# Three-branch attention layers and a mixture of experts on one core: the output gate's modulation weights are loaded and summed during attention instead of among the projections

## The chip, the cores and the metric

The kernel runs on one core of one Trainium2 chip, in float32. The metric is the device time of one execution in microseconds (us), as the median of three runs. TensorE (PE) multiplies and writes into eight banks of on-chip memory (`banks` in the trace), everything else lies in one large buffer (`arena`). VectorE (DVE), ScalarE (ACT) and GpSimd (POOL) work beside it, and SyncE (SP) issues nearly all of the weight loads.

## The reference, cut to what matters

Two layers of the first kind (`DEPTH = 2`), then one block of a second kind that ends in a mixture of experts. The change touches only the two layers. `x` is 256 tokens by 1024, and `gate` is one row of 1024 numbers for all tokens.

```python
for l in range(DEPTH):
    mod = c_act @ w_ada[l] + b_ada[l]
    shift, scale, gate = [m[:, None, :] for m in split_cols(mod, (D, D, D))]
    h = rms_norm(x, g_pre[l]) * (1.0 + scale) + shift
    (cq, ckv, kr, za, qb_, kb_, vb_, zb, qc, kc, vc, zc, gcols) = split_cols(h @ w_in[l], IN_SPLITS)
    o_a = (mla_branch(cq, ckv, kr, g_q[l], w_uq[l], g_kv[l], w_ukv[l], cos, sin)
           * jax.nn.silu(za)) @ w_o_mla[l]
    o_b = (swa_branch(qb_, kb_, vb_, sink[l], swa_bias) * jax.nn.silu(zb)) @ w_o_swa[l]
    o_c = (diff_branch(qc, kc, vc, ..., rel_bias, lam_init) * jax.nn.silu(zc)) @ w_o_diff[l]
    g = jax.nn.sigmoid(gcols).reshape(B, S, N_BRANCH, D)
    y = (g[:, :, 0] * o_a + g[:, :, 1] * o_b + g[:, :, 2] * o_c) @ w_out[l]
    x = x + gate * rms_norm(y, g_post[l])
```

## The kernel before

**A layer has four stages.** First x is transposed and scaled (jobs `xT`). Then come the projections that attention needs (jobs `cq`, `ckv`, `qb`, `kb`, `vb`, `qr`, `qn`, `qc`, `kn`, `kc`, `v`, `vc`). Then attention itself, 24 units of which each is a head or half of one (8 sliding-window, 8 differential, 8 latent), runs in 25 ticks (`TICKS`). In each tick PE does the scores, transposes or values of a unit and in between a piece of the fill: the jobs from `z` to the last `g`, with `ada` and `modT`, the next layer's shift and scale. `share` deals the fill out over the ticks by a cost per job, a quarter of a `z` or `g` job being the smallest piece. Last come the output products (`wo`, `wout`) and the new x. In the first layer the projections lie at 42 to 147 us of the trace and attention at 148 to 327 us, in the second at 408 to 505 us and from 506 us on.

**Jobs and banks.** `layer_jobs` writes the order of the jobs on PE by hand. Job number n uses one of three banks in turn; it waits until the engine that read job n-3 has let the bank go.

**Loads and slots.** `layer_loads` writes the order in which SP issues the weight loads (L776), each of at most 128 partitions x 2048 numbers (1 MB), into a ring of six slots. Load i goes into the slot of load i-6, so SP waits until the last job that uses load i-6 is done (`LAST_USER`), and since SP works in order, all loads behind it wait too. A projection of 512 columns takes two loads, for input rows 0 to 511 and 512 to 1023.

**The gate.** `gate` is made on DVE, not on PE: four loads (`mods_now`, two for each half of the rows, 4 MB in all) are multiplied row tile by row tile with the condition's column and summed into `mrow` (`gate_rows`, L719 and L725: 16 instructions of 128x512). Half 1 is summed before DVE reads `qr`, half 2 after it has copied `kc` 0. The slots of these loads come free by DVE's signals `gate_read` and `gate_sum`. Two PE jobs `gate` (L858, a product with a matrix of ones) then add over the partitions, and DVE turns the result with `row_b` (bias) and `row_g` (the post-norm weights) into `G1` (L1370, L1372), which is used at the layer's end. `row_g` lies in `pT`, the buffer into which attention copies transposed probabilities, so G1 must be done before attention.

**Softmax chain in a tick.** DVE scales the scores and takes the maximum (`before_exp`, L1404 to L1410), ACT does the exponentials (L1129), DVE normalises (L1420 to L1445), PE transposes in the next tick (L956). Scores of units u and u+1 (L946) are computed together in even ticks and wait until the exponentials of unit u-1 are done.

Of the kernel before, what the change touches and what calls it, by code (L numbers as in the profile page):

```python
# [42 lines left out]
def layer_loads():  # L43
# [10 lines left out]
    for c in (4, 5):  # L54
        loads.append(("mods_now", 0, 4, 512 * c, 512))
# [26 lines left out]
def layer_jobs():  # L82

    jobs = []
    for i in range(4):
# [7 lines left out]
    i += 4  # L93
    uq, qc, ukv, kc, vc = (i,), (i + 1, i + 2), (i + 3,), (i + 6, i + 7), (i + 8, i + 9)
    i += 10
    jobs += [("qr", 0, uq), ("qn", 0, uq), ("qc", 0, qc), ("qn", 1, uq), ("qc", 1, qc), ("kn", 0, ukv),
             ("kc", 0, kc), ("kn", 1, ukv), ("kc", 1, kc), ("v", 0, ukv), ("v", 1, ukv), ("gate", 0, ()),
             ("vc", 0, vc), ("gate", 1, ()), ("vc", 1, vc)]
    for z in range(3):
        jobs += [("z", 2 * z, (i, i + 1)), ("z", 2 * z + 1, (i, i + 1))]  # L100
        i += 2
# [43 lines left out]
TICKS = NU + 1  # L145

# [12 lines left out]
def share(jobs, first, last, parts, t):  # L159
# [3 lines left out]
    for j in range(first, last):  # L163
        cost = {"ada": 1 / 3, "mod": 1 / 3, "modT": 1 / 10, "modT2": 1 / 10}.get(jobs[j][0])
# [20 lines left out]
def fill_jobs(t):  # L185

    return finished(fill_shares(t))
# [317 lines left out]
def blocks_kernel(nc, A, out):  # L505
# [4 lines left out]
    with ExitStack() as ctx:  # L510
# [82 lines left out]
        row_b, row_g = spare[:, 0:D], pT  # L593
# [115 lines left out]
        def gate_rows(dve, loads, half, turns, cond, acc):  # L709
# [70 lines left out]
        def _(pe):  # L780
# [31 lines left out]
            for l in range(LAYERS):  # L812
# [25 lines left out]
                def job(j, quarters=WHOLE):  # L838
# [17 lines left out]
                    elif kind == "gate":  # L856
                        pe.wait_ge(gate_sum.sem, gate_sum.at(l, n + 1))
                        mm = pe.matmul(b, C("ones"), mrow[:, 512 * n:512 * n + 512], start=True, stop=True)  # L858
# [184 lines left out]
        def _(act):  # L1043
# [16 lines left out]
            act.dma_start(row_b, A["b_ada"][0:1, 2 * D:3 * D].to_broadcast([P, D])).then_inc(rows_in, 16)  # L1060
            act.dma_start(row_g, A["g_post"][0:1, :].to_broadcast([P, D])).then_inc(rows_in, 16)

            for l in range(LAYERS):
# [18 lines left out]
                copy_job(j, cq, bank_of(l, j))  # L1082
                j = JOB_OF["ckv", 0]
# [55 lines left out]
                for t in range(TICKS):  # L1139
# [10 lines left out]
                    for j in fill_jobs(t):  # L1150
                        kind, n, _ = JOBS[j]
                        if kind == "modT":
                            continue
# [20 lines left out]
                if l < LAYERS - 1:  # L1174
                    act.dma_start(lv, A["lvecs"][l + 1]).then_inc(lv_in, 16)
                    act.dma_start(row_b, A["b_ada"][l + 1:l + 2, 2 * D:3 * D].to_broadcast([P, D])).then_inc(rows_in, 16)
                    act.dma_start(row_g, A["g_post"][l + 1:l + 2, :].to_broadcast([P, D])).then_inc(rows_in, 16)
# [1580 lines left out]
```

## Time and profile before

| | |
|---|---|
| time, median of three runs (lowest to highest) | 2347.01 us (2346.2 to 2348.6) |
| the profiled execution: its time, its span in the trace | 2345.47 us, 2343.7 us |
| PE matmul busy | 1808.4 us, 77% |
| DVE busy | 524.9 us, 22% |
| ACT busy | 287.4 us, 12% |
| the chain that ended last, shares of the span | PE 48%, DMA 46%, DVE 3% |
| PE waiting for `w_in` loads at L830, whole run | 7.6 us |

The page cuts the span into 40 slices of 58.6 us. In slices 2 to 19, PE is busy for nine tenths or more nearly throughout and the DMA queues for two to seven tenths. From slice 20 on it is the other way round: the experts' weights stream in at 427 to 430 GB/s with the DMA nine tenths busy, and PE waits. The chain that ended last shows the same: PE lines up to about 1110 us, then loads of the experts' weights. A view "in order of time" lists start, duration, what; a bracket gives the idle time before it and who ended it. In these views one matmul of float32 shows as two records, so a job of 16 matmuls is x32.

### The profile page before, as it was taken

The page shows a single profiled execution, that of the slowest core. Times are in us where ns is not written, and L with a number is a line of the kernel's source. Part 1 is how long each engine was busy: PE and PEld are TensorE (multiplying, and loading weights), DVE is VectorE, ACT ScalarE, POOL GpSimd, SP SyncE. Part 2 cuts the span into 40 slices and gives each one's busy share as a digit, 9 for nine tenths or more (in the row PEclk, how much of TensorE's full clock was granted, in tenths as well). Part 3 has the DMA queues.
Part 4 walks back from the last instruction along what each step waited for, and adds up shares of the span by engine and source line. Part 5 has one row for each costly group of instructions (what it writes and reads, how often), then busy time and mean ns, then how long its engine had stood idle before and what let it go on. Part 6 is the DMA issues. An engine that isn't in the chain of part 4 may idle for free.

```text
span 2343.7 us, 23974 instructions
## 1 busy us (share of the span) xinstructions
PE 1808.4 (77%) x10388; PEld 1018.3 (43%) x10388; DVE 524.9 (22%) x1136; ACT 287.4 (12%) x710; POOL 61.9 (3%) x101
## 2 busy tenths in 40 slices
PE   6999999999999999989666575656666665666666
PEld 3767785867786677554212121212221222222212
DVE  1234323234313337753000010000010000000001
ACT  1122211113220112311000000000000000000001
POOL 1000000000000300110000000000000000000000
PEclk9999999999999999999878787877787877788778
DMA  9664453443464341378999999999999999999996
GB/s 301 214 202 144 171 181 112 150 175 138 171 222 135 123 144 37 106 289 363 427 428 425 429 429 427 425 430 428 427 427 429 428 427 428 429 427 427 429 428 265
DMA packets 126223, 714.38 MB, mean 305 GB/s; under 512 B 11545, under 2 KB 16089, under 8 KB 96303
## 3 DMA queue, kind: packets, MB, share of 16 engines
q1 hardware_dynamic: 117568, 697.07, 73.4%
q10 hardware_dynamic: 6279, 9.88, 1.3%
q0 software_dynamic: 2272, 5.90, 1.1%
q8 instruction: 83, 1.36, 0.2%
q14 instruction: 21, 0.17, 0.0%
HBM read 709.02 MB, written 3.80 MB: 304 GB/s over the span
## 4 chain that ended last, share of the span: by engine, by line
PE 48%; DMA 46%; DVE 3%; SPq 1%; ACT 1%; issue 1%; POOL 0%; DVEq 0%; ACTq 0%
DMA arena<-in_w_up_dram 22%; DMA arena<-in_w_down_dram 20%; PE banks L830 14%; PE banks L2547 5%; PE banks L1723 4%; PE banks L918 4%; PE banks L1732 3%; PE banks L2579 2%; PE banks L926 2%; DMA arena<-in_w_mods_dram 2%; PE banks L2587 2%; PE banks L835 2%; DMA arena<-in_w_in_dram 1%; PE banks L946 1%; PE banks L1765 1%; PE banks L974 1%
## 5 line engine op out<-in xcount | busy, mean ns | idle before, releaser
L2547 PE MATMUL banks<-arena 128*32 128x512 f32 (+2 forms) x3072 | 418.1, 682 | 330.1 <-DMA arena<-in_w_up_dram 330.1
L2547 PEld LDWEIGHTS banks<-arena 128*32 128x32 f32 x3072 | 131.5, 132 | 587.1 <-issue 579.7
L830 PE MATMUL banks<-arena 128*128 128x256 f32 x1536 | 346.7, 382 | 7.6 <-DMA arena<-in_w_in_dram 7.6
L830 PEld LDWEIGHTS banks<-arena 128*128 128x128 f32 x1536 | 287.9, 191 | 50.3 <-DMA arena<-in_w_in_dram 8.8
L2579 PE MATMUL banks<-arena 128*32 128x512 f32 x1280 | 205.0, 792 | 95.2 <-DMA arena<-in_w_down_dram 95.2
L2675 DVE SCALAR_TENSOR_TENSOR arena<-arena,banks 64x512 f32<-64x512 f32 (+1 forms) x48 | 30.5, 635 | 517.9 <-ACT arena L2598 516.9
L2579 PEld LDWEIGHTS banks<-arena 128*32 128x32 f32 x1280 | 44.3, 132 | 229.9 <-DMA arena<-in_w_down_dram 129.7
L2598 ACT ACTIVATE arena<-banks 64x512 f32<-64x512 f32 (+1 forms) x48 | 26.6, 555 | 818.9 <-PE banks L2547 817.6
L1723 PE MATMUL banks<-arena 128*128 128x256 f32 x512 | 113.7, 380 | 1.4 <-DVE arena L2120 0.7
L1723 PEld LDWEIGHTS banks<-arena 128*128 128x128 f32 x512 | 95.9, 190 | 16.1 <-issue 3.8
L2682 DVE COPY arena<-banks 128x512 f32<-128x512 f32 x16 | 11.1, 692 | 350.1 <-PE banks L2588 350.1
L918 PE MATMUL banks<-arena 128*128 128x256 f32 x384 | 83.4, 379 | 1.7 <-DVE arena L1482 1.7
L918 PEld LDWEIGHTS banks<-arena 128*128 128x128 f32 x384 | 72.8, 190 | 12.3 <-issue 2.5
L1732 PE MATMUL banks<-arena 128*128 128x512 f32 x160 | 69.8, 593 | 0.0
L2668 DVE COPY arena<-banks 128x256 f32<-128x256 f32 x16 | 6.8, 425 | 258.4 <-PE banks L2485 258.4
L2498 PE MATMUL banks<-arena 128*128 128x512 f32 x128 | 60.0, 611 | 0.8 <-ACT arena L2612 0.8
L926 PE MATMUL banks<-arena 128*128 128x512 f32 x128 | 55.4, 593 | 3.5 <-DVE arena L1501 3.5
L2551 PE MATMUL banks<-arena 128*32 128x128 f32 x512 | 55.3, 295 | 0.0
L2516 PE MATMUL banks<-arena 64*128 64x64 f32 x176 | 30.1, 289 | 31.0 <-DVE arena L2677 31.0
L2612 ACT COPY arena<-banks 128x512 f32<-128x512 f32 x16 | 9.4, 585 | 327.9 <-PE banks L2588 327.9
L1129 ACT ACTIVATE arena<-arena 128x256 f32<-128x256 f32 x64 | 32.0, 500 | 118.1 <-DVE arena L1410 67.9
L2551 PEld LDWEIGHTS banks<-arena 128*32 128x32 f32 x512 | 34.4, 123 | 27.0 <-issue 8.9
(334 smaller groups left out, 1688.6 us busy)
## 6 DMA issues: line engine op xcount, KB each, us to landing
arena<-in_w_gate_dram SPq DMA_DIRECT2D x60, 2752.0 KB, 35.7
arena<-in_w_up_dram SPq DMA_DIRECT2D x60, 2752.0 KB, 32.7
arena<-in_w_down_dram SPq DMA_DIRECT2D x64, 2048.0 KB, 32.0
arena<-in_w_in_dram SPq DMA_DIRECT2D x68, 1024.0 KB, 7.7
arena<-in_w_mods_dram SPq DMA_DIRECT2D x48, 1024.0 KB, 7.3
arena<-in_w_down_dram SPq DMA_DIRECT2D x32, 1024.0 KB, 27.0
arena<-in_w_out_dram SPq DMA_DIRECT2D x12, 1024.0 KB, 5.7
arena<-in_w_gate_dram SPq DMA_DIRECT2D x8, 1376.0 KB, 9.6
```

The source lines that it names most:

```text
L830: mm = pe.matmul(b[:, i * S:i * S + S], w, rhs[:, kt, :], start=kt == 0, stop=kt == 7)
L835: mm = pe.matmul(outp, cols(slot(i0 + kt // 4)[:, kt % 4, :]), rhs[:, kt, :], start=kt == 0, stop=kt == 7)
L918: mm = pe.matmul(b[:, i * S:i * S + S], w[:, k, c:c + P], zv[:, 4 * br + k, :], start=k == 0, stop=k == 3)
L926: mm = pe.matmul(b, hTv[:, kt, t * P:t * P + P], slot(loads[0] + kt // 4)[:, kt % 4, :], start=kt == 0, stop=kt == 7)
L1129: ins = nc.scalar.activation(Ev[:, u % 3, t * S:t * S + S], src, ACT.Exp, bias=nmx[:, u % 3, t:t + 1], scale=QK ** -0.5 if kind == "mla" e ...
L1723: mm = pe.matmul(b[:, i * S:i * S + S], slot(loads[kt // 4])[:, kt % 4, c0:c0 + P], rhs[:, kt, :], start=kt == 0, stop=kt == 7)
L1732: mm = pe.matmul(b, lhs[:, kt, (n % 2) * P:(n % 2) * P + P], slot(loads[kt // 4])[:, kt % 4, :], start=kt == 0, stop=kt == 7)
L2498: mm = pe.matmul(acc[2 * t + c], GT[:, e % 2, t * P:t * P + P], Y[:, 512 * c:512 * c + 512], start=e == 0, stop=e == NE - 1, skip_group_ch ...
L2547: mm = pe.matmul(bank[pc][32 * g:32 * g + 32, 0:w_], xsT[:, kt, CAP * e4:CAP * e4 + CAP], (wg if g < 2 else wu)[:, c:c + w_], start=kt == ...
L2551: mm = pe.matmul(bank[pc][32 * g:32 * g + 32, LAST - c0:w], xsT[:, kt, CAP * e4:CAP * e4 + CAP], (wg if g < 2 else wu)[:, FF - 64:FF].unsq ...
L2579: mm = pe.matmul(bank[c][32 * g:32 * g + 32, :], hTv3[:, j, 32 * hf:32 * hf + 32], w_[:, 512 * c:512 * c + 512], start=(g, c) not in start ...
L2587: pe.matmul(bank[c][0:32, :], hTv3[:, 10, 0:32], lo[:, 512 * c:512 * c + 512], start=False, stop=True)
```

## The change

It moves the four `mods_now` loads from among the projections to behind the loads of `zb` and `zc`; moves the summation on DVE into attention's ticks 1, 2 (half 1) and 4, 5 (half 2); moves the two `gate` jobs on PE behind the `z` jobs, into the fill (tick 7); and moves the making of G1 there too. The sums are kept in `xn[:, 0:D]`, the buffer of the normalised x, which is idle between `xT` and the layer's end, and `row_g` in its other half. So `mrow` and `pT` are free of them, and both rows are loaded in each layer by ACT after its copy of `cq`, instead of before the first layer and after attention.

```diff
@@ layer_loads
     chunk("w_in", D, COL["kb"], 256)
-    for c in (4, 5):
-        loads.append(("mods_now", 0, 4, 512 * c, 512))
     loads.append(("w_uq", 0, 2, 0, MLA_H * QK))
     chunk("w_in", D, COL["qc"], 512)
     loads.append(("w_ukv", 0, 1, 0, MLA_H * (NOPE + VD)))
-    for c in (4, 5):
-        loads.append(("mods_now", 512, 4, 512 * c, 512))
...
     for z in ("zb", "zc", "za"):
         chunk("w_in", D, COL[z], 512)
+        if z != "za":
+            for c in (4, 5):
+                loads.append(("mods_now", 0 if z == "zb" else 512, 4, 512 * c, 512))
@@ layer_jobs
-             ("kc", 0, kc), ("kn", 1, ukv), ("kc", 1, kc), ("v", 0, ukv), ("v", 1, ukv), ("gate", 0, ()),
-             ("vc", 0, vc), ("gate", 1, ()), ("vc", 1, vc)]
+             ("kc", 0, kc), ("kn", 1, ukv), ("kc", 1, kc), ("v", 0, ukv), ("v", 1, ukv),
+             ("vc", 0, vc), ("vc", 1, vc)]
...
+    jobs += [("gate", n, ()) for n in range(2)]
...
+GATE_TICKS = {1: (1, (0, 1)), 2: (1, (2, 3)), 4: (2, (0, 1)), 5: (2, (2, 3))}
@@ share
-        cost = {"ada": 1 / 3, "mod": 1 / 3, "modT": 1 / 10, "modT2": 1 / 10}.get(jobs[j][0])
+        cost = {"ada": 1 / 3, "mod": 1 / 3, "modT": 1 / 10, "modT2": 1 / 10, "gate": 1 / 10}.get(jobs[j][0])
@@ buffers
-        row_b, row_g = spare[:, 0:D], pT
+        row_b, row_g, gate_acc = spare[:, 0:D], xn[:, D:2 * D], xn[:, 0:D]
@@ gate_rows
-            for i in both:
-                dve.wait_ge(ring_full[(MOD_LOADS + i) % RING], 16 * (turns + (MOD_LOADS + i) // RING + 1))
-            for k in range(4):
+            if part[0] == 0:
+                for i in both:
+                    dve.wait_ge(ring_full[(MOD_LOADS + i) % RING], 16 * (turns + (MOD_LOADS + i) // RING + 1))
+            for k in part:
@@ ACT, in each layer between its copy of cq and its copy of ckv (and no longer ahead of
@@ layer 0 and behind attention)
+                act.dma_start(row_b, A["b_ada"][l:l + 1, 2 * D:3 * D].to_broadcast([P, D])).then_inc(rows_in, 16)
+                act.dma_start(row_g, A["g_post"][l:l + 1, :].to_broadcast([P, D])).then_inc(rows_in, 16)
@@ DVE, projections
-                gate_rows(dve, GATE_LOADS, 1, l * (NLOAD // RING), 0, mrow)
...
-                        if n == 0:
-                            gate_rows(dve, GATE_LOADS, 2, l * (NLOAD // RING), 0, mrow)
@@ DVE, in each tick, behind before_exp and normalise
+                    if t in GATE_TICKS:
+                        half, part = GATE_TICKS[t]
+                        gate_rows(dve, GATE_LOADS, half, l * (NLOAD // RING), 0, gate_acc, part)
                     for j in fill_jobs(t):
...
+                        if kind == "gate":
+                            a = slice(512 * n, 512 * n + 512)
+                            dve.wait_ge(job_done.sem, made(l, j))
+                            dve.wait_ge(rows_in, 32 * l + 32)
+                            nc.vector.tensor_tensor(row_b[:, a], bank_of(l, j), row_b[:, a], ALU.add).then_inc(v_own.sem, v_own.up())
+                            dve.wait_ge(v_own.sem, v_own.last())
+                            nc.vector.scalar_tensor_tensor(G1[:, a], row_b[:, a], 0.5, row_g[:, a], ALU.mult, ALU.mult).then_inc(reader(l, j), 1)
```

The loads on SP's queue, from the first layer's `kb` (128x4x256) to the loads of the first `g` jobs, before:

```order
L776 DMA arena<-in_w_in_dram 128x4x256 x2
L776 DMA arena<-in_w_mods_dram 128x4x512 x2
L776 DMA arena<-in_w_uq_dram 128x2x768
L776 DMA arena<-in_w_in_dram 128x4x512 x2
L776 DMA arena<-in_w_ukv_dram 128x1024
L776 DMA arena<-in_w_mods_dram 128x4x512 x2
L776 DMA arena<-in_w_in_dram 128x4x512 x12
```

and in the changed kernel:

```order
L778 DMA arena<-in_w_in_dram 128x4x256 x2
L778 DMA arena<-in_w_uq_dram 128x2x768
L778 DMA arena<-in_w_in_dram 128x4x512 x2
L778 DMA arena<-in_w_ukv_dram 128x1024
L778 DMA arena<-in_w_in_dram 128x4x512 x6
L778 DMA arena<-in_w_mods_dram 128x4x512 x2
L778 DMA arena<-in_w_in_dram 128x4x512 x2
L778 DMA arena<-in_w_mods_dram 128x4x512 x2
L778 DMA arena<-in_w_in_dram 128x4x512 x4
```

The x6 are `kc`, `vc` and `zb`; then stand the gate's half 1, `zc`, the gate's half 2, `za` and the first `g`. So every load from `w_uq` to `zb` now goes into the slot of a load that stands six useful loads ahead of it.

DVE in tick 1 and the start of tick 2 of the first layer's attention, before (score scaling, maximum, normalising, then the `z` job's gating at L1469):

```order
L1404 SCALAR_TENSOR_TENSOR arena<-banks,arena 128x256
L1405 SCALAR_TENSOR_TENSOR arena<-banks,arena 128x256
L1407 TENSOR_REDUCE arena<-arena 128x2
L1410 TENSOR_SCALAR arena<-arena 128x2
L1420 TENSOR_TENSOR arena<-arena 128x2
L1422 RECIPROCAL arena<-arena 128x2
L1445 TENSOR_SCALAR arena<-arena 128x256 x2
L1469 SCALAR_TENSOR_TENSOR arena<-arena,banks 128x512
L1404 SCALAR_TENSOR_TENSOR arena<-banks,arena 128x256
```

and in the changed kernel:

```order
L1393 SCALAR_TENSOR_TENSOR arena<-banks,arena 128x256
L1394 SCALAR_TENSOR_TENSOR arena<-banks,arena 128x256
L1396 TENSOR_REDUCE arena<-arena 128x2
L1399 TENSOR_SCALAR arena<-arena 128x2
L1409 TENSOR_TENSOR arena<-arena 128x2
L1411 RECIPROCAL arena<-arena 128x2
L1434 TENSOR_SCALAR arena<-arena 128x256 x2
L721 TENSOR_SCALAR arena<-arena 128x512 x2
L727 SCALAR_TENSOR_TENSOR arena<-arena 128x512 x2
L1468 SCALAR_TENSOR_TENSOR arena<-arena,banks 128x512
L1393 SCALAR_TENSOR_TENSOR arena<-banks,arena 128x256
```

Four instructions of the gate's sum (L721, L727) stand behind the unit's normalising and ahead of the `z` job's gating. The same holds in ticks 2, 4 and 5, with four of L727 each.

PE at the end of the projections, before (`v` at L906, `gate` at L858, `vc` at L886, the first scores at L946):

```order
L906 MATMUL banks<-arena 128x512 x2
L858 MATMUL banks<-arena 128x512
L886 MATMUL banks<-arena 128x512 x8
L858 MATMUL banks<-arena 128x512
L886 MATMUL banks<-arena 128x512 x8
L946 MATMUL banks<-arena 128x256 x4
```

and in the changed kernel:

```order
L908 MATMUL banks<-arena 128x512 x2
L888 MATMUL banks<-arena 128x512 x16
L948 MATMUL banks<-arena 128x256 x4
```

The two `gate` jobs have left this place; they stand in tick 7, behind the last `z` job and ahead of the scores of tick 8.

## Rows read from the trace of the kernel before

**Rows 1.** The page, part 2: PE's busy tenths in 40 slices of the span

```profile
PE   6999999999999999989666575656666665666666
```

**Rows 2.** PE in order of time, layer 0's projections: start, us, what, [idle before]

```profile
86.76 1.89 PE L830 MATMUL banks<-arena 128*128 128x256 f32 x8
91.91 5.45 PE L830 MATMUL banks<-arena 128*128 128x256 f32 x24 [3.25 <-DMA arena<-in_w_in_dram]
97.19 1.90 PE L896 MATMUL banks<-arena 128*128 128x256 f32 x8
98.92 7.07 PE L830 MATMUL banks<-arena 128*128 128x256 f32 x32
...
106.94 1.99 PE L830 MATMUL banks<-arena 128*128 128x256 f32 x8
...
116.52 1.08 PE L902 MATMUL banks<-arena 128*64 128x256 f32 x8
...
127.12 3.60 PE L886 MATMUL banks<-arena 128*128 128x512 f32 x8
134.41 5.40 PE L886 MATMUL banks<-arena 128*128 128x512 f32 x8 [3.70 <-DMA arena<-in_w_in_dram]
139.65 1.02 PE L858 MATMUL banks<-arena 128*128 128x512 f32 x2
140.51 7.03 PE L886 MATMUL banks<-arena 128*128 128x512 f32 x16
```

**Rows 3.** The same view, layer 1's projections

```profile
467.67 1.99 PE L830 MATMUL banks<-arena 128*128 128x256 f32 x8
471.79 7.13 PE L830 MATMUL banks<-arena 128*128 128x256 f32 x24 [2.12 <-DMA arena<-in_w_in_dram]
478.85 1.08 PE L902 MATMUL banks<-arena 128*64 128x256 f32 x8
...
489.45 3.59 PE L886 MATMUL banks<-arena 128*128 128x512 f32 x8
...
497.51 1.02 PE L858 MATMUL banks<-arena 128*128 128x512 f32 x2
```

**Rows 4.** Stretches: length, busy PE, PEld, DVE, ACT, POOL, granted clock, DMA share, GB/s

```profile
134.00:137.00 3.00, 2.58 (x4) 1.07 (x5) 0.00 (x0) 0.00 (x0) 0.00 (x0) 0.61 1.05 385
...
470.00:475.00 5.00, 3.21 (x9) 2.60 (x10) 0.00 (x0) 0.00 (x0) 0.00 (x0) 0.76 0.81 304
```

**Rows 5.** SP's queue in order of time: the two loads of `qc`, layer 0

```profile
73.94 9.13 SPq L776 DMA_DIRECT2D arena<-in_w_in_dram  x2
```

**Rows 6.** The line of the weight loads (L776), 60 to 160 us: issue to landing

```profile
DMA to landing us min/median/max: 4.8/7.6/14.9
```

**Rows 7.** DVE in order of time: the gate's sums in layer 0

```profile
88.14 4.06 DVE L725 SCALAR_TENSOR_TENSOR arena<-arena 128x512 f32<-128x512 f32 x6
...
117.35 5.39 DVE L725 SCALAR_TENSOR_TENSOR arena<-arena 128x512 f32<-128x512 f32 x8
```

**Rows 8.** DVE in order of time, attention: tick 2 starts, tick 2 ends

```profile
161.54 0.42 DVE L1404 SCALAR_TENSOR_TENSOR arena<-banks,arena 128x256 f32<-128x256 f32 x1 [3.20 <-PE banks L946]
...
168.45 0.42 DVE L1482 SCALAR_TENSOR_TENSOR arena<-banks,arena 128x256 f32<-128x256 f32 x1 [1.53 <-PE banks L974]
```

**Rows 9.** ACT in order of time: unit 3's last exponential (tick 3)

```profile
171.55 0.28 ACT L1133 ACTIVATE arena<-arena 128x2 f32<-128x2 f32 x1
```

**Rows 10.** PE in order of time: the scores of tick 4, which wait for it

```profile
174.00 1.14 PE L946 MATMUL banks<-arena 64*128 64x256 f32 x8
```

**Rows 11.** POOL in order of time: the root made at the end of tick 13

```profile
244.94 0.70 POOL L1225 TENSOR_TENSOR arena<-arena 128x2 f32<-128x2 f32 x1 [13.85 <-DVE arena L1458]
```

**Rows 12.** PE in order of time: the product in tick 14 that needs it

```profile
247.41 0.61 PE L1030 MATMUL banks<-arena 128*128 128x128 f32 x4
```

**Rows 13.** ACT in order of time: its copy of `ckv` in layer 0

```profile
56.31 0.37 ACT L1085 COPY arena<-banks 128x256 f32<-128x256 f32 x1 [6.43 <-PE banks L835]
```

**Rows 14.** What SP's queue waited for, 850 to 1200 us: us in total, times, longest

```profile
SPq L2441 <- PE banks L1765: 27.8, 1, 27.8
```

More of the change, by code:

```diff
@@ L92, in layer_jobs @@
     jobs += [("kb", 0, (i, i + 1)), ("vb", 0, (i, i + 1))]
[L93 to L95 removed]
+    i += 2
+    uq, qc, ukv, kc, vc = (i,), (i + 1, i + 2), (i + 3,), (i + 4, i + 5), (i + 6, i + 7)
+    i += 8
     jobs += [("qr", 0, uq), ("qn", 0, uq), ("qc", 0, qc), ("qn", 1, uq), ("qc", 1, qc), ("kn", 0, ukv),
[L97 to L98 removed]
+             ("kc", 0, kc), ("kn", 1, ukv), ("kc", 1, kc), ("v", 0, ukv), ("v", 1, ukv),
+             ("vc", 0, vc), ("vc", 1, vc)]
     for z in range(3):
         jobs += [("z", 2 * z, (i, i + 1)), ("z", 2 * z + 1, (i, i + 1))]
[L101 removed]
+        i += 4 if z < 2 else 2
+    jobs += [("gate", n, ()) for n in range(2)]
     for g in range(6):
@@ L707, in taken, with gate_rows @@
             return place(l, j) // BANKS + 2
-        def gate_rows(dve, loads, half, turns, cond, acc):
+        def gate_rows(dve, loads, half, turns, cond, acc, part=range(4)):
             both = [i for i, n in sorted(loads.items()) if n == half]
-            for i in both:
-                dve.wait_ge(ring_full[(MOD_LOADS + i) % RING], 16 * (turns + (MOD_LOADS + i) // RING + 1))
-            for k in range(4):
+            if part[0] == 0:
+                for i in both:
+                    dve.wait_ge(ring_full[(MOD_LOADS + i) % RING], 16 * (turns + (MOD_LOADS + i) // RING + 1))
+            for k in part:
                 for c, i in enumerate(both):
@@ L857, in job @@
                         pe.wait_ge(gate_sum.sem, gate_sum.at(l, n + 1))
-                        mm = pe.matmul(b, C("ones"), mrow[:, 512 * n:512 * n + 512], start=True, stop=True)
+                        mm = pe.matmul(b, C("ones"), gate_acc[:, 512 * n:512 * n + 512], start=True, stop=True)
                     elif kind == "xT":
@@ L1151, in _ @@
                         kind, n, _ = JOBS[j]
-                        if kind == "modT":
+                        if kind in ("modT", "gate"):
                             continue
@@ L1360, in _ @@
                 dve.wait_ge(v_own.sem, v_own.last())
-                gate_rows(dve, GATE_LOADS, 1, l * (NLOAD // RING), 0, mrow)
-                dve.wait_ge(rows_in, 32 * l + 32)
                 for kind, n, _ in MIDDLE:
-                    if kind not in ("kc", "qr", "gate"):
+                    if kind not in ("kc", "qr"):
                         continue
@@ L1367, in _ @@
                     dve.wait_ge(job_done.sem, made(l, j))
-                    if kind == "gate":
-                        a = slice(512 * n, 512 * n + 512)
-                        nc.vector.tensor_tensor(row_b[:, a], bank_of(l, j), row_b[:, a], ALU.add).then_inc(v_own.sem, v_own.up())
-                        dve.wait_ge(v_own.sem, v_own.last())
-                        nc.vector.scalar_tensor_tensor(G1[:, a], row_b[:, a], 0.5, row_g[:, a], ALU.mult, ALU.mult).then_inc(reader(l, j), 1)
-                        continue
                     if kind == "kc":
                         nc.vector.tensor_copy(kcT[:, 512 * n:512 * n + 512], bank_of(l, j)).then_inc(reader(l, j), 1)
-                        if n == 0:
-                            gate_rows(dve, GATE_LOADS, 2, l * (NLOAD // RING), 0, mrow)
                         continue
```

4 lines of the change are left out of this document (removed).

## The prediction, made before the changed kernel was run

> **What bounds the kernel now.** I read the page's slices first: PE is busy nine tenths of nearly all of slices 1 to 18, then only five to seven tenths [rows 1]. So up to about 1110 us PE's order of work is the path, and behind it the experts' weights stream in. The question for the tail is whether a head start reaches the end. SP's first loads of those weights wait 27.8 us for PE's line L1765 [rows 14]: the stream is started by PE's progress, not by a clock of its own. Whatever PE gains in the layers, the stream should start that much earlier, and the end moves one for one.
>
> Second, PE in order of time over the projections. In layer 0 it stands still three times in the middle of a job, always for the job's second `w_in` load: in `qc` 0 (3.25 us, behind 86.76), `kc` 0 (behind 106.94) and `vc` 0 (3.70 us) [rows 2]. Layer 1 shows two, in `kc` 0 (2.12 us) and `vc` 0 [rows 3]. Attention behind it has nearly no waits.
>
> Third, why those loads are late. It isn't bandwidth: landing takes 4.8 us at best, 7.6 in the middle [rows 6]. It is the slots. The two `w_in` loads of `qc` take 9.13 us to issue [rows 5]: the first goes out at 73.94, when `qb` is done, and the second at 73.94 + 9.13 = 83.1, because its slot belongs to `kb` and `vb` must be done with it. Its job resumes at 91.91 [rows 2]. The second load of `vc` waits for the slot of `w_ukv`, free when `v` 1 is done just before 127.1, and its job resumes at 134.41 [rows 2]. The code says why the slots are short: two of the six hold gate weights, first half 1, then half 2, and these come free only by DVE.
>
> **Part 1, the stalls go.** I price each job by its start and the start of the next row, against a job without a stall: 7.07 us for L830 x32, 7.03 for `vc` x16 [rows 2]. `qc` 0: 97.19 - 86.76 = 10.43, too long by 3.36. `kc` 0: 116.52 - 106.94 = 9.58, by 2.51. `vc` 0: 139.65 - 127.12 = 12.53, by 5.50. Layer 0: 11.37 us. Layer 1 [rows 3]: `kc` 0 478.85 - 467.67 = 11.18, by 4.11; `vc` 0 497.51 - 489.45 = 8.06, by 1.03; together 5.14 us. The sum is **16.5 us**.
>
> It holds more than the waits, since the granted clock was 0.61 in 134 to 137 us and 0.76 in 470 to 475 [rows 4]: behind a stall some matmuls ran at the lower level of 1.2 GHz. Eight records took 5.40 instead of 3.60 us, and 24 took 7.13 instead of 5.45 [rows 2, 3]. Behind the 3.25 us wait in `qc` 0, the 24 records took 5.45, no such loss. The Trainium skill (TensorE: Matmul & The Clock Gate, Why this matters for your kernels) asks for matmul bursts without long idle gaps and says that a gap long enough drops the clock. The trace agrees for 3.70 us and not for 3.25, while 2.12 us in layer 1 did cost it; priced by the rule alone, the 3.25 us gap would add some 1.7 us to the sum, which the row denies.
>
> **Do the new slots come free in time?** I walk the new order with the old times, less what is saved by then. The second `qc` load now takes a slot of `qb`, free at 73.9 us [rows 5], and is needed at 86.76 + 1.89 = 88.7 [rows 2]: 14.8 us. Both `kc` loads take `kb`'s slots, free at 83.1 [rows 5], and the first is needed at 106.94 - 3.36 = 103.6: 20 us. The second `vc` load takes a slot of `qc`, free when `qc` 1 is done at 98.92 + 7.07 - 3.36 = 102.6, and is needed at 127.12 - 5.87 - 0.86 + 3.6 = 124.0 (5.87 for the two stalls before it, 0.86 for the `gate` job that leaves, 140.51 - 139.65 [rows 2]): 21 us. The second `zb` load takes `w_ukv`'s slot at about 120.4 and is needed some 17 us later, behind two `vc` jobs of 7.03, the first scores and a first quarter job. The worst landing was 14.9 [rows 6]. Projections: no stall left.
>
> **Part 2, the gate loads.** The ticks' times first, by the old clock: DVE's tick 1 ends at 161.54 - 3.20 = 158.3 [rows 8]; PE's tick 2 begins 1.14 us ahead of 161.54, at 160.4, and its tick 4 at 174.00 [rows 10], so a tick is 6.8 us. Now half 1: it is issued behind `zb` at 121 us, and DVE asks for it at 158 less the 13.1 us by which attention starts earlier (11.4 and the two `gate` jobs' 1.7), so at 145: 24 us for three loads. Half 2 takes `zb`'s slots when `z` 1 is done in tick 2, two quarter jobs and the transposes behind the scores, at 160.4 + 1.1 + 0.6 + 3.6 = 165.7, and is wanted in tick 4 some 5 us behind its scores, at 179: 13 us. `za` waits for DVE's `gate_read` at the end of its tick 2 (168.5) and is needed by PE in tick 5, at 174.0 + 6.8 + 0.6 + 1.8 = 183.2: 15 us. These two are the tight ones, with nearly twice the median landing.
>
> **Part 3, the sums on DVE.** Eight instructions take 5.39 us [rows 7], so a tick gets 2.7 us. Nothing is added, it is moved; in the projections it hid behind PE. In tick 1 the 3.20 us idle takes it [rows 8]. In tick 2 the 1.53 us idle and 0.6 us more take all but 0.6 us of it [rows 8], so unit 3's exponential ends at 171.83 + 0.6 = 172.4 [rows 9]; the scores that need it start at 174.00 [rows 10]. Cover left: 1.6 us. Ticks 4 and 5 hold the same instructions, and the new deal of the fill gives PE a quarter job more in tick 5. **Cost 0**; without the cover a tick would cost up to 2.7 us.
>
> **Part 4, PE's gate jobs and G1.** The same two jobs, moved: 0. In tick 7 DVE adds four steps of about 0.68 us (4.06 / 6 [rows 7]), 2.7 us ahead of tick 8, whose exponentials no PE work needs before tick 9: 0. DVE also waits there for the two rows, which ACT has issued more than 100 us before.
>
> **Part 5, the row loads on ACT.** They stand between the copies of `cq` and `ckv`, where ACT idles 6.43 us for PE [rows 13]; two issues under 1 us hide there: 0. Their 1 MB now travels with the `w_uq` and `qc` loads, which the Trainium skill (DMA: Bandwidth & Descriptors, Issuing engines are not separate DMA queues) says share the same 16 engines whoever issues. No row prices that here; by it `qc` would land a few us later, inside its 15 us.
>
> **Part 6, the fill is dealt anew.** The costs of two `gate` jobs shift pieces between ticks. Tick 13 loses one quarter job, 1.8 us of PE. At its end PE needs a root that POOL makes at 244.94 + 0.70 = 245.64, for L1030 at 247.41 [rows 11, 12]. Less 1.8 that is 245.6, so a wait of 0.1 to 0.4 us, in both layers. I take **0.5 us lost**; bounds 0 and 2 (a whole POOL step and its signals in each layer).
>
> **The sum.** 16.5 - 0.5 = 16.0 us off the profiled 2345.47: 2329.5. The median is 1.54 us above the profiled run, so **2331 us**.
>
> **Rivals.** *A new late load in attention.* `za` or gate half 2 misses by a landing near 14.9 us [rows 6], PE stalls some 2 us in tick 4 or 5 and pays the clock's 1.8 us again, in both layers: about 8 us lost, **2339 us**. For: SP's order puts DVE's `gate_read` ahead of all later loads. Against: both have 13 us or more and the median is 7.6 [rows 6].
>
> *The stalls only move (the change doesn't do what it says).* If transfer speed and not slots set the arrivals, dropping 4 MB out of the stretch would still leave waits, since `zb` follows at once: half of the gain, 2339, or none, **2347**. Against: the 9.13 us issue [rows 5] is a slot wait.
>
> *Slower: the sums enter the softmax chain.* All 16 sums and the four steps of G1 on the path would be 20 x 0.68 = 13.5 us a layer, 27 in both, less 16.0: **2358 us**. It decides when DVE's delay at tick 4's scores passes the 1.6 us left, or the gate's weights land more than 24 us after issue, so that DVE stands in tick 1 with the `z` gating and unit 2's score scaling queued behind it, and PE's transposes of unit 2 in tick 3 wait for those. Against: DVE's idle in each tick.
>
> **How the numbers follow.** Forecast 0.80 (2327 to 2335: the sum with part 6's bounds, and 1 to 2 us for run to run and for a stall priced by one execution). New late load 0.10 (2335 to 2343). Stalls move 0.06 (2339 to 2347). Sums on the path 0.04. The range 2326 to 2339 holds the forecast and most of the second case. A measurement of this kernel can tell about 0.2%, 4.7 us, from no change: faster 0.93, same 0.04, slower 0.03.
>
> **What would show it.** Right: no wait of PE for `in_w_in_dram` in either layer's projections, granted clock 1.00 there, attention starting near 135 us instead of 148 in layer 0 and near 488 instead of 506 in layer 1, and the experts' first loads 16 us earlier. Wrong: waits of L830 in ticks 4 or 5 for a load, of L946 for ACT or DVE in ticks 2 to 6, or an end that moved less than the experts' first load.

## The result, and the profile after

| | before | after |
|---|---|---|
| median (lowest to highest) | 2347.81 us (2346.2 to 2348.95, 4 runs) | 2329.27 us (2327.31 to 2330.87, 4 runs) |
| ratio after to before, 95% interval | | 0.9922 (0.991 to 0.9934) |
| span of the profiled execution | 2343.7 us | 2327.4 us |
| PE matmul busy | 1808.4 us | 1809.7 us |
| DVE, ACT busy | 524.9, 287.4 us | 523.9, 287.3 us |

The forecast was 2331 us. The medians are 18.5 us apart, the two profiled executions 16.3 us, where the prediction's sum was 16.0. No engine has less work (PE's busy time differs by 1.3 us, DVE's by 1.0): what went is idle time.

PE in the page's slices, to be held against [rows 1]. Only four slices have another digit, each by one tenth and all in the experts' part: at 58 us a slice, waits of 1 to 4 us don't show, and these digits alone would say that nothing happened:

```profile
PE   6999999999999999989666566656665666666666
```

PE's costliest line in the layers, from the page. It does the same 1536 records in 343.4 us (346.7 before, where some of them ran at the lower clock), and the idle time ahead of it, 7.6 us for loads before, is 0:

```profile
L832 PE MATMUL banks<-arena 128*128 128x256 f32 x1536 | 343.4, 380 | 0.0
```

PE in order of time over the projections of layer 0 (start, duration, what), which answers to [rows 2]:

```profile
86.51 7.07 PE L832 MATMUL banks<-arena 128*128 128x256 f32 x32
...
103.17 7.17 PE L832 MATMUL banks<-arena 128*128 128x256 f32 x32
...
118.30 1.88 PE L908 MATMUL banks<-arena 128*128 128x512 f32 x4
120.01 13.90 PE L888 MATMUL banks<-arena 128*128 128x512 f32 x32
134.69 1.14 PE L948 MATMUL banks<-arena 64*128 64x256 f32 x8 [0.78 <-ACT arena L1067]
```

`qc` 0 (86.51) is one unbroken row of 32 records (before 8, a wait, 24), so is `kc` 0 (103.17), and `vc` 0 and 1 are one row of 13.90 us. The first scores start at 134.69 instead of 148.32. Layer 1, against [rows 3] (`kc` 0 lies at 455.87, 7.17 us, unbroken too):

```profile
472.72 13.90 PE L888 MATMUL banks<-arena 128*128 128x512 f32 x32
487.39 1.14 PE L948 MATMUL banks<-arena 64*128 64x256 f32 x8 [0.78 <-ACT arena L1067]
```

And the granted clock (the column PEclk, here the 1.00 behind POOL's) over both stretches, which was 0.61 and 0.76 in places before [rows 4]:

```profile
core 0: us, PE busy (x) PEld busy (x) DVE busy (x) ACT busy (x) POOL busy (x), PEclk, DMA share, GB/s
60.00:135.00 75.00, 74.22 (x337) 56.16 (x337) 11.74 (x20) 11.87 (x21) 4.85 (x7) 1.00 0.68 205
425.00:490.00 65.00, 64.22 (x290) 48.03 (x289) 13.10 (x23) 9.22 (x16) 0.00 (x0) 1.00 0.48 164
```

How much earlier each point of the program is reached, from the views in order of time (* not in the rows above or in those of before):

| | before | after | earlier by |
|---|---|---|---|
| layer 0, first scores | 148.32* | 134.69 | 13.6 |
| layer 0, first `wo` | 327.68* | 315.87* | 11.8 |
| layer 1, first scores | 506.18* | 487.39 | 18.8 |
| layer 1, first `wo` | 685.54* | 668.58* | 17.0 |
| experts' first load issued | 1041.00* | 1024.10 | 16.9 |
| end of the span | 2343.7 | 2327.4 | 16.3 |

The experts' first load, before and after, in SP's queue in order of time:

```profile
1041.00 0.34 SPq L2441 DMA_DIRECT2D arena<-in_w_gate_dram  x1
1024.10 0.34 SPq L2440 DMA_DIRECT2D arena<-in_w_gate_dram  x1
```

Each attention is 1.8 us longer, which is the two `gate` jobs moved into it.

### The profile page after: what moved, and what is told of

The parts are those of the page before. It is cut to its first block, busy times and chain, and to the rows that moved or that the text cites. A ratio compares the mean times of both kernels' runs of the same rounds, so it can differ in the third digit from the quotient of the medians.

```text
span 2327.4 us, 23978 instructions
## 1 busy us (share of the span) xinstructions
PE 1809.7 (78%) x10388; PEld 1019.3 (44%) x10388; DVE 523.9 (23%) x1136; ACT 287.3 (12%) x710; POOL 61.8 (3%) x101
## 4 chain that ended last, share of the span: by engine, by line
PE 49%; DMA 44%; DVE 3%; SPq 1%; ACT 1%; issue 1%; POOL 0%; DVEq 0%; ACTq 0%
DMA arena<-in_w_up_dram 22%; DMA arena<-in_w_down_dram 21%; PE banks L832 14%; PE banks L2546 5%; PE banks L1722 4%; PE banks L920 4%; PE banks L1731 3%; PE banks L928 2%; PE banks L2578 2%; DMA arena<-in_w_mods_dram 2%; PE banks L2586 2%; PE banks L837 2%; PE banks L948 1%; PE banks L1764 1%; PE banks L888 1%; PE banks L976 1%
## 5 line engine op out<-in xcount | busy, mean ns | idle before, releaser
L832 PE MATMUL banks<-arena 128*128 128x256 f32 x1536 | 343.4, 380 | 0.0
L832 PEld LDWEIGHTS banks<-arena 128*128 128x128 f32 x1536 | 287.3, 190 | 39.7 <-issue 3.0
L920 PEld LDWEIGHTS banks<-arena 128*128 128x128 f32 x384 | 72.8, 190 | 12.3 <-issue 2.5
```

The source lines that it names most:

```text
L832: mm = pe.matmul(b[:, i * S:i * S + S], w, rhs[:, kt, :], start=kt == 0, stop=kt == 7)
L920: mm = pe.matmul(b[:, i * S:i * S + S], w[:, k, c:c + P], zv[:, 4 * br + k, :], start=k == 0, stop=k == 3)
```

## The experiments

**Theory:** the gate loads cost time by the places that they take in the ring's order, not by their bytes and not by DVE's lateness. **Rivals:** transfer speed; DVE's late release; and, for what the new place costs, a softmax chain on the edge. Ratios are to the kernel before, run on the same chip beside it; differences to after in microseconds are between medians that may come from different chips.

**1. Same places, next to no bytes.** The gate weights are cut to 16 of 512 columns, so most of them are left out.

```diff
@@ before: SP's loop over the loads
+                    if name == "mods_now":
+                        w = 16
                     sp.dma_start(view(ring[:, s_, 0:k * w], k, w), ...)
```

> The kernel before, except that each of the four gate loads of a layer brings 16 columns instead of 512 (32 KB instead of 1 MB); the slots, their order and DVE's sums stay, so most of the gate's weights are left out. Theory (slots: a load waits until the load six places ahead of it is used up, and gate loads take two of the six places): the second halves of qc, kc and vc still land late, PE still waits some 9 us in layer 0 and 3 us in layer 1, and the time is within 3 us of before. Rival (transfer speed: 4 MB more in the projections delay the others): PE's waits for w_in go, and the time falls by 10 to 17 us.

Measured: 2348.36 us, ratio 1.0003 (0.9993 to 1.0012). PE's waits, from the view of waits in 40 to 700 us:

```profile
PE banks L832 <- DMA arena<-in_w_in_dram: 7.6, 3, 3.4
PE banks L888 <- DMA arena<-in_w_in_dram: 4.7, 2, 3.9
```

Four MB fewer per layer and all five waits are still there, 12.3 us of them. It is the places.

**2. The bytes without the places.** The kernel after, with 3.5 MB per layer of loads that nobody reads, into idle buffers outside the ring, issued by SP among the projections' loads; ACT and DVE wait for them ahead of attention.

```diff
@@ after: SP's loop, ahead of load 6 and of load 10 of each layer
+                    if i == 6:
+                        for dst in (G[:, 4096:6144], zs[:, 0:2048]):
+                            sp.dma_start(view(dst, 4, 512), dram("mods_now", l, 0, 4, 2048, 512)).then_inc(extra_in, 16)
+                    if i == 10:
+                        for dst in (zs[:, 2048:3072], pT, mrow):
+                            sp.dma_start(view(dst, 2, 512), dram("mods_now", l, 512, 2, 2048, 512)).then_inc(extra_in, 16)
```

> The changed kernel with 3.5 MB of extra loads per layer that nobody reads, issued where the gate's halves stood before (2 MB behind kb's loads, 1.5 MB behind w_ukv's), into buffers that attention fills only later, so into no slot of the ring. Theory (slots): PE has no wait for w_in in the projections, attention starts within 1 us of the changed kernel's 134.7 us, and the time is within 2 us of it. Rival (transfer speed): waits of several us come back in qc or kc, and the time rises by 5 to 17 us.

Measured: 2329.0 us, ratio 0.9922 (0.9906 to 0.9937), the same as after. The windows (DMA share is the second last column), first of this kernel, then of after:

```profile
55.00:65.00 10.00, 10.00 (x48) 7.42 (x47) 0.16 (x1) 1.67 (x4) 1.04 (x1) 1.00 0.94 295
...
85.00:95.00 10.00, 10.00 (x48) 8.79 (x47) 6.97 (x9) 1.76 (x3) 0.00 (x0) 1.00 0.94 312
```

```profile
55.00:65.00 10.00, 10.00 (x48) 7.50 (x47) 0.16 (x1) 1.67 (x4) 2.62 (x3) 1.00 0.74 256
...
85.00:95.00 10.00, 10.00 (x48) 8.79 (x47) 6.83 (x9) 1.76 (x3) 0.00 (x0) 1.00 0.70 232
```

The DMA engines are busy for 0.94 of both stretches, after's for 0.74 and 0.70, and PE is full in them; it has no wait for `w_in` in the layers, and the first scores start at 134.82. With 1 and 2 the rival of transfer speed is out from both sides.

**3. One half back.** The kernel after with the two loads of half 1 back behind `kb`'s and summed there; half 2 stays in attention, and the job indices and `GATE_TICKS` follow.

```diff
@@ after: layer_loads
     chunk("w_in", D, COL["kb"], 256)
+    for c in (4, 5):
+        loads.append(("mods_now", 0, 4, 512 * c, 512))
...
-        if z != "za":
+        if z == "zc":
             for c in (4, 5):
-                loads.append(("mods_now", 0 if z == "zb" else 512, 4, 512 * c, 512))
+                loads.append(("mods_now", 512, 4, 512 * c, 512))
@@ DVE, projections
+                gate_rows(dve, GATE_LOADS, 1, l * (NLOAD // RING), 0, gate_acc)
```

> The changed kernel with half 1 of the gate put back: its two loads stand behind kb's again and DVE sums it ahead of qr; only half 2 is loaded behind zc and summed in ticks 4 and 5. Theory (slots): load i waits for load i-6, so the second qc load waits for vb again and PE waits 3 to 4 us in qc 0 of layer 0 (start to start 10.4 instead of 7.0 us), nothing in kc 0 or vc 0 and nothing in layer 1; the time is 3.4 us above the changed kernel. Rival (each half costs the same): half of the gain is lost, 8 us above it.

Measured: 2336.86 us, ratio 0.995 (0.9933 to 0.9967), 7.6 us above after. The only wait of PE for `w_in` in the layers, and the row behind it, in order of time:

```profile
86.86 1.89 PE L834 MATMUL banks<-arena 128*128 128x256 f32 x8
93.41 7.65 PE L834 MATMUL banks<-arena 128*128 128x256 f32 x24 [4.66 <-DMA arena<-in_w_in_dram]
100.90 1.90 PE L900 MATMUL banks<-arena 128*128 128x256 f32 x8
```

The place was foreseen (`qc` 0, and none in `kc` and `vc`), the price was not: 100.90 - 86.86 = 14.04, too long by 7.0 where [rows 2] gave 3.36. The job resumed 1.5 us later than there (93.41 against 91.91), after a wait of 4.66 us, which is longer than `qc` 0's in any execution of before or of experiments 1 and 4 (3.15 to 3.61) and wasn't explained, and the 24 records behind took 7.65 instead of 5.45. These 7.0 us are nearly the 7.6 measured, so half 1 alone makes `qc` 0's stall, and the other four waits need half 2's places (whether half 2 makes them alone wasn't run). The price differs between executions: one of the four runs took 2332.4 us, the others 2336.8 to 2337.1.

**4. Free the same places earlier.** The kernel before, with half 1's sums ahead of a wait in DVE's program, so that its slots come free earlier. No work is left out.

```diff
@@ before: DVE, projections
+                gate_rows(dve, GATE_LOADS, 1, l * (NLOAD // RING), 0, mrow)
                 dve.wait_ge(misc_done.sem, misc_done.at(l, 2))
...
-                gate_rows(dve, GATE_LOADS, 1, l * (NLOAD // RING), 0, mrow)
```

> The kernel before, except that DVE sums half 1 of the gate as soon as it has landed (near 62 us, where DVE is idle) instead of at 87 us, so that its two slots come free some 20 us earlier. Rival (the slots come free late because DVE is late): the waits of qc and kc in layer 0 go and the time falls by 5 to 9 us. Theory (the places in the order count, not how long DVE holds them): the late second loads wait for vb, qc 1 and v 1, which are PE's jobs, so all three waits stay and the time is within 2 us of before.

Measured: 2348.4 us, ratio 1.0002 (0.9993 to 1.0012). The wait in `qc` 0 stays, as do the other four (PE waits 12.2 us for `w_in` in all, as in before):

```profile
91.69 7.13 PE L830 MATMUL banks<-arena 128*128 128x256 f32 x24 [3.15 <-DMA arena<-in_w_in_dram]
```

It isn't how late DVE reads half 1. The late loads wait for the slots of `kb`, `qc` and `w_ukv`, six places back in the order, as the prediction's walk says for the first and the last of them.

**5. Fill two waits.** The kernel before, with matmuls that nobody reads between the halves of `vc` 0 (layer 0) and `kc` 0 (layer 1), to price the low clock behind a wait by itself.

```diff
@@ before: PE, job vc
                         for kt in range(8):
+                            if kt == 4 and l == 0 and n == 0:
+                                turn_over(pe, SB[0], 4)
@@ PE, job kc 0 of layer 1, between the quarters of its first and second load
+                            turn_over(pe, SB[0], 2)
```

> The kernel before with matmuls whose result nobody reads put into two of the waits: four of 128x512 (3.6 us at full clock) in vc 0 of layer 0, whose wait was 3.7 us, and two (1.8 us) in kc 0 of layer 1, whose wait was 2.1 us. Theory (1.7 us of each of these two stalls was the lower clock behind it, not the wait): the clock stays at 1.00, the matmuls behind the waits take 3.6 instead of 5.4 us and 5.4 instead of 7.1 us, and attention of layer 1 starts 3.5 us earlier than before. Rival (only the wait itself costs, the slow records are those of a late load): no change, within 0.5 us in the trace.

Measured: 2345.52 us, ratio 0.9989 (0.998 to 0.9998). The rows at the two places:

```profile
130.74 3.60 PE L748 MATMUL banks<-arena 128*128 128x512 f32 x8
134.38 3.70 PE L890 MATMUL banks<-arena 128*128 128x512 f32 x8
...
467.77 1.88 PE L748 MATMUL banks<-arena 128*128 128x512 f32 x4
470.07 5.45 PE L832 MATMUL banks<-arena 128*128 128x256 f32 x24 [0.42 <-DMA arena<-in_w_in_dram]
```

L748 is the filler. The loads come no earlier after their job's start (7.07 and 4.13 us, before 7.29 and 4.12), but the records behind take 3.70 instead of 5.40 and 5.45 instead of 7.13 [rows 2, 3]: 1.70 + 1.68 = 3.4 us is the clock's part of these two stalls. The experts' first load goes out 3.5 us earlier in the profile (1037.52 us), while the median moved by 2.2. The waits in `qc` 0 and `kc` 0 of layer 0 were left open, and the 24 records behind each took 5.45 us, as in the execution of [rows 2]:

```profile
92.10 5.45 PE L832 MATMUL banks<-arena 128*128 128x256 f32 x24 [3.26 <-DMA arena<-in_w_in_dram]
```

**6. Fill all five waits.** The same in all five, to see what the clock costs in sum.

```diff
@@ before: PE, in pair between the two loads (as in 5), and its call by qb, qc and kc
+                        mm = pair(b, loads[0], n * 256, hTv, fill={("qc", 0, 0): 3, ("kc", 0, 0): 2, ("kc", 0, 1): 2}.get((kind, n, l), 0))
@@ PE, job vc
                         for kt in range(8):
+                            if kt == 4 and n == 0:
+                                turn_over(pe, SB[0], (4, 1)[l])
```

> The kernel before with matmuls whose result nobody reads in all five waits of the projections (layer 0: three of 128x512 in qc 0, two in kc 0, four in vc 0; layer 1: two in kc 0, one in vc 0; 0.9 us each at full clock, at most as long as the wait was). The waits for loads end when they did, so only the clock behind them can change. Theory (behind each wait the clock drops in some executions and not in others, and this is why the changed kernel gained 18.3 us in the median where one execution's stalls came to 16.5): no matmul behind a wait runs at the lower clock, and the time is 4 to 6 us below before, near 2343 us. Rival (the clock costs only what the first profile showed, 3.4 us, and the rest of the gain is elsewhere): 2 to 3.5 us below.

Measured: 2346.68 us, ratio 0.9994 (0.9985 to 1.0003): less than either side expected. The rows behind the two waits that 5 had left alone, and the load that came late instead, near the experts:

```profile
92.20 5.45 PE L832 MATMUL banks<-arena 128*128 128x256 f32 x24 [0.77 <-DMA arena<-in_w_in_dram]
...
111.51 5.45 PE L832 MATMUL banks<-arena 128*128 128x256 f32 x24 [0.57 <-DMA arena<-in_w_in_dram]
...
1021.18 1.07 PE L1694 MATMUL banks<-arena 128*32 128x512 f32 x8 [2.46 <-DMA arena<-in_w_mods_dram]
1023.64 1.94 PE L1694 MATMUL banks<-arena 128*32 128x512 f32 x8 [1.40 <-DMA arena<-in_w_mods_dram]
```

The clock loss behind the five waits is gone, and layer 1's scores start at 504.21 us. But from there to the experts' first load it takes 537.7 us, where the profiled executions of before (three) and of experiments 1, 4 and 5 take 534.7 to 535.0. PE waited 4.7 us for loads at L1694, in before 3.2, and 8 records behind took 1.94 us where they take 1.07: 2.4 of the 2.9 us that this execution gave back shortly ahead of the experts. Why that load is late here and not in 5, whose layer 1 scores start still earlier (502.85 us), wasn't found, and one profile doesn't say what the other ten runs did. So what the clock behind the waits costs in the median stays open.

**7. The kernel before, twice more**, each with a profile, to see how much a stall differs between executions.

```diff
-# ---- launch: one core
+# ---- launch 1: one core
```

> The kernel before, unchanged, for a further execution's trace. Theory (which waits are followed by the lower clock differs between executions): the same five waits at the same places within 0.3 us, but qc 0 and kc 0 of layer 0 take 7.1 instead of 5.4 us for the 24 records behind the wait in at least one of this and its twin. Rival (the clock follows the length of the wait alone): qc 0 and kc 0 of layer 0 take 5.4 us behind their waits as before.

> The kernel before, unchanged, a second further trace; theory and rival as for its twin.

Measured: 2347.4 and 2349.74 us, spans 2345.6 and 2347.9. `qc` 0 in each of the two:

```profile
86.65 1.89 PE L830 MATMUL banks<-arena 128*128 128x256 f32 x8
91.79 7.13 PE L830 MATMUL banks<-arena 128*128 128x256 f32 x24 [3.25 <-DMA arena<-in_w_in_dram]
98.76 1.90 PE L896 MATMUL banks<-arena 128*128 128x256 f32 x8
```

```profile
87.28 1.89 PE L830 MATMUL banks<-arena 128*128 128x256 f32 x8
92.78 8.45 PE L830 MATMUL banks<-arena 128*128 128x256 f32 x24 [3.61 <-DMA arena<-in_w_in_dram]
101.07 1.90 PE L896 MATMUL banks<-arena 128*128 128x256 f32 x8
```

The same program and, in the first, the same wait of 3.25 us, but the 24 records that took 5.45 us in the execution of [rows 2] take 7.13; behind 3.61 us in the second they take 8.45. It is the clock: in 92 to 96 us the granted one was 1.00 in the execution of [rows 2], and here, in the first of the two:

```profile
92.00:96.00 4.00, 4.00 (x12) 3.21 (x12) 3.94 (x8) 0.00 (x0) 0.00 (x0) 0.57 0.72 226
```

Too long by, each job priced as in Part 1:

| us | `qc` 0 | `kc` 0 | `vc` 0 | L1 `kc` 0 | L1 `vc` 0 | sum |
|---|---|---|---|---|---|---|
| before, profiled | 3.36 | 2.51 | 5.50 | 4.11 | 1.03 | 16.5 |
| before again, 1 | 5.04 | 4.18 | 5.02 | 4.40 | 1.11 | 19.8 |
| before again, 2 | 6.72 | 4.22 | 5.32 | 4.20 | 0.97 | 21.4 |
| experiment 1 | 5.17 | 4.08 | 6.90 | 2.41 | 0.92 | 19.5 |
| experiment 4 | 4.94 | 4.21 | 5.18 | 4.16 | 1.17 | 19.7 |
| experiment 5, `vc` 0 and L1 `kc` 0 filled | 3.37 | 2.51 | 3.58 | 2.44 | 1.10 | 13.0 |
| experiment 6, filled | 3.45 | 2.59 | 3.57 | 3.78 | 0.95 | 14.3 |

The profiled execution of before was the cheapest of the five that left all waits open. Of the six that left `qc` 0 and `kc` 0 open, four paid the lower clock in both and two (before, experiment 5) in neither.

**8. The sums made dearer.** The kernel after, with each sum on DVE preceded by one, then two additions of 128x512 that nobody reads. This asks how near the slower rival was.

```diff
@@ after: gate_rows, in each step in attention (range(1); range(2) in the second kernel)
+                    if len(part) == 2:
+                        for _ in range(1):
+                            nc.vector.tensor_tensor(mrow[:, 512 * c:512 * c + 512], w, w, ALU.add).then_inc(dup.sem, dup.up())
+                            dve.wait_ge(dup.sem, dup.last())
```

> The changed kernel with each of the gate's sums in attention preceded by one more DVE instruction of the same size whose result nobody reads (0.7 us each, 2.8 us more in ticks 1, 2, 4 and 5). Theory (DVE has 1.1 us idle left ahead of tick 2, and 1.75 us between unit 3's exponential and the scores of tick 4): DVE comes 1.7 us late out of tick 1 and 4.5 us late out of tick 2, so PE waits 2.5 to 3 us ahead of the scores of tick 4 in each layer and little elsewhere; 5 to 7 us above the changed kernel. Rival (there is room for all): within 1 us. Rival (every DVE instruction in attention is on the path): 11 us a layer, 22 us above.

> The same with two more instructions for each sum (5.6 us more in each of the four ticks). Theory: DVE comes 4.5 us late out of tick 1 and 10 us late out of tick 2; beyond the cover every further us costs one, so PE waits some 8 us by the scores of tick 4 and again some 4 to 8 us by the scores of tick 6 in each layer: 24 to 32 us above the changed kernel. Rival (room for all): within 1 us.

Measured: 2340.83 us, ratio 0.9971 (0.996 to 0.9982), 11.5 us above after; and 2366.9 us, ratio 1.008 (1.0063 to 1.0097), 37.6 above. PE's waits in 40 to 700 us, first with one addition more, then with two:

```profile
PE banks L954 <- ACT arena L1140: 5.9, 2, 3.1
PE banks L982 <- ACT arena L1156: 4.7, 2, 2.9
```

```profile
PE banks L982 <- ACT arena L1156: 18.2, 4, 6.6
PE banks L954 <- ACT arena L1140: 9.2, 3, 4.5
```

L954 is the scores that wait for an exponential, the path of Part 3. L982 is the values, which wait for ACT's copy of the transposed probabilities, and this path the prediction didn't have. PE's transposes of that unit, and then ACT in order of time with one addition more shows why it is there:

```profile
179.64 0.66 PE L964 MATMUL banks<-arena 128*128 128x128 f32 x4
```

```profile
186.60 0.51 ACT L1136 ACTIVATE arena<-arena 128x256 f32<-128x256 f32 x1 [7.92 <-DVE arena L1405]
...
187.79 0.56 ACT L1156 COPY arena<-banks 128x512 f32<-128x512 f32 x1
```

The copy stands behind the next unit's exponential on ACT, and that one waits 7.92 us for DVE. So a late DVE holds back the copy, and with it PE's values of a unit whose transposes ended at 180.3 us. PE there:

```profile
188.40 1.09 PE L982 MATMUL banks<-arena 128*64 128x256 f32 x8 [2.93 <-ACT arena L1156]
...
190.33 4.88 PE L838 MATMUL banks<-arena 128*128 128x256 f32 x16
```

The 16 records of L838 cost 4.88 us instead of some 3.6 (in before, 16 records of the same job at 526.59 us). The waits for the exponential, 5.9 us, are what the expectation had (5 to 7); the other two, 4.7 us, and the low clock behind all four it left out. This execution is 14.2 us behind after's at the experts' first load (1038.31 us), and 11.4 at the end. With two additions the expectation (24 to 32 us) was too low in the same way: 18.2 of the 27.4 us of waits are L982's. The slower rival's mechanism exists, and becomes slower than before between one and two more additions per sum: not at the DVE time that the change really moves.

**9. PE's last waits for readers moved.** The kernel after, with the wait ahead of the first scores (0.78 us in each layer) put behind them, to tick 1.

```diff
@@ after: PE, attention
-                for j in range(FIRST_FILL - BANKS, FIRST_FILL):
-                    pe.wait_ge(reader(l, j), taken(l, j))
                 for t in range(TICKS):
                     if t < NU and t % 2 == 0:
                         scores(t)
+                    if t == 1:
+                        for j in range(FIRST_FILL - BANKS, FIRST_FILL):
+                            pe.wait_ge(reader(l, j), taken(l, j))
```

> The changed kernel, but PE waits for the readers of the last three projection jobs (v 1, vc 0, vc 1) in tick 1 instead of ahead of tick 0, since the first scores and the first z job need none of them. Theory (the wait of 0.78 us for ACT's copy of vc 1 is the only thing between the last projection and the first scores): both waits go, 1.6 us below the changed kernel, 2327.7 us. Rival (the z job's bank or the scores wait for the same copy anyway): no change.

Measured: 2327.35 us, ratio 0.9913 (0.9898 to 0.9928). The first scores, in order of time:

```profile
134.07 1.14 PE L948 MATMUL banks<-arena 64*128 64x256 f32 x8
```

The wait is gone in both layers. The median is 1.9 us below after's, but the two intervals overlap, so the trace shows the gain and the times don't settle it. It has the lowest median here.

## Why the prediction was right, point by point

**Part 1, the stalls go: right in place, under-priced.** All five waits went, the clock is 1.00, the first scores moved by 13.6 us (13.1 foreseen; 0.25 us of the rest is an earlier start of `qc` 0, and 0.3 that the price set start to start against durations: 7.07 us in `qc` 0, where after's lasts 93.42 - 86.51 = 6.91 to the next row's start) and to 487.39 in layer 1 (488 foreseen). Against the profiled execution the 16.5 us hold (16.9 by start to start throughout). The mis-sized term is the step "I price each job by its start", from one execution: in four of the five others that left `qc` 0 and `kc` 0 open, the same stalls cost 19.5 to 21.4 us, since the lower clock that was missing behind these two in [rows 2] was there. The spans of those four are 1.4 to 4.2 us longer than the profiled one's, which fits medians that are 18.5 us apart where the two profiles are 16.3. It isn't shown that all of the rest is this: experiment 6 took the clock's part away, and its median fell by only 0.9 us. "1.54 us above the profiled run" was the other slip. In after the profiled run (2329.22 us) lies at the median (2329.27), so this gap, which may have been part of the stalls that go, wasn't there to be added: 2331 is too high by about that much.

With it falls what the prediction read from one 3.25 us wait against the rule of the Trainium skill (TensorE: Matmul & The Clock Gate, Why this matters for your kernels), which asks for bursts without long idle gaps since a long enough gap drops the clock. Of the other five executions with a wait there, four did pay: 1.7 us behind 3.15, 3.25 and 3.39 us (7.13 instead of 5.45), 3.0 us behind 3.61; the fifth, behind 3.26, did not. The rule's price for that gap, some 1.7 us more, is what half of the six show, and the row with which it was denied was one draw.

**Slots: right**, by four runs: nearly no bytes in the same places changed nothing, 3.5 MB more outside the ring changed nothing, earlier sums of half 1 changed nothing, and half 1 back in its places cost 7.6 us, with `qc` 0's the only stall.

**Part 2, gate loads: right.** DVE's steps in ticks 1 and 4 start behind its own work, with no wait for a load (144.02 and 165.74 us in the view of DVE), and PE has no wait for `za`. PE's waits in attention of layer 0 (135 to 320 us) are of three kinds, none for a load, with the times that they had before:

```profile
PE banks L1025 <- ACT arena L1172: 1.4, 3, 0.5
PE banks L920 <- DVE arena L1481: 0.8, 1, 0.8
PE banks L948 <- ACT arena L1067: 0.8, 1, 0.8
```

So the rival of a new late load didn't come about.

**Part 3, sums on DVE, cost 0: right, with half of the reasons.** Behind the first scores, no row of L948 waits for anything. Tick 4 in order of time, PE's scores and then DVE's sums, behind which its next step follows without a wait:

```profile
160.37 1.14 PE L948 MATMUL banks<-arena 64*128 64x256 f32 x8
```

```profile
165.74 2.73 DVE L727 SCALAR_TENSOR_TENSOR arena<-arena 128x512 f32<-128x512 f32 x4
168.45 0.42 DVE L1481 SCALAR_TENSOR_TENSOR arena<-banks,arena 128x256 f32<-128x256 f32 x1
```

But beyond the cover the text's "up to 2.7 us a tick", which is some 22 us for four ticks in two layers, isn't a bound: sixteen additions a layer cost 11.5 us, the next sixteen 26. The second path, through ACT's copy to PE's values, was missing in the walk.

**Part 4, right** at 0: the `gate` jobs' 1.7 us only moved from the projections into attention, and each attention is longer by 1.8. **Part 6, 0.5 us lost: not there.** Of the 1.8 us, 1.7 are the `gate` jobs, so 0.1 is left for it, and no wait for POOL is among those above.

**Part 5, right at 0, wrong in its term.** "Two issues under 1 us" were 4.5 us in layer 0:

```profile
49.04 0.35 ACTq L1082 DMA_DIRECT2D arena<-in_b_ada_dram  x1
49.42 4.17 ACTq L1083 DMA_DIRECT2D arena<-in_g_post_dram  x1
56.06 0.37 ACT L1086 COPY arena<-banks 128x256 f32<-128x256 f32 x1 [6.43 <-PE banks L837]
```

They still end at 53.6 us, 2.5 us ahead of the copy, whose idle time is the 6.43 us that it was [rows 13]. Part 5's step counted what hides them rightly and had no row for what they cost.

**The tail: right.** The head start of 16.9 us at the experts' first load arrives as 16.3 at the end. From that load to the end twelve profiled executions (all but the dearest sums) take 1300.5 to 1303.4 us, in no order that goes with the change, and the 0.6 is within that. That 16.3 comes so near to the sum's 16.0 is in part luck: 0.4 us more in the stalls and the 0.5 us of part 6 that wasn't lost make the 16.9, and the 0.6 of the tail took most of it back.

## What to carry to other kernels

Count the places between a load and the one whose slot it takes: in a ring, a load costs its place to everything behind it. Here neither next to no bytes nor an earlier reader of half 1 changed that. Price a stall from several executions, and ask of the gap between a profiled run and the median whether it lies in the stalls that you remove, before you add it to the time after. When work is moved under cover on an engine, follow every reader of that engine, those too that only queue behind one on a third engine.

## What the runs showed of the hardware that was not expected

The clock behind a wait differs between executions, and the length of the wait alone doesn't tell it. Behind waits of 2.1 to 3.6 us, the same 24 records took 5.45, 7.13 or 8.45 us where PE had run the same program up to there: behind 3.25 us in `qc` 0 once 5.45 and once 7.13, and behind 2.1 us in `kc` 0 of layer 1 once 5.45 (2.10 us, experiment 1) and once 7.13 (2.12 us, before). With the wait filled by unread matmuls they took 5.45 each time. What decides it wasn't found. How far whole runs lie apart doesn't follow from it: with all five waits filled, eleven runs still lie within 8.1 us (2341.99 to 2350.05), and the 15 of before beside them within 6.8.

A DMA issue on ACT's queue took 4.17 us in layer 0 and 0.45 us for the same line in layer 1 (in order of time at 403 us). What held it wasn't tried.
